# Four closings of a two-layer backbone rebuilt: gate rows from SBUF, units prepared early, token tiles in a pipeline

## The chip, the cores and the metric

The kernel runs on one core of a Trainium2 chip. The metric is the device time of one execution in microseconds (us), the median of several runs; lower is better. Engines are named as in the profile: PE (TensorE), DVE (VectorE), ACT (ScalarE), POOL (GpSimd), SP (SyncE, which issues most DMAs).

## The reference, cut to what matters

Two layers work on 128 context tokens and 256 latent tokens, 384 rows of 2048 values. Context and latent rows have different modulation vectors (group 0 and group 1).

```python
def trunk_layer(x, cvec, ctx_kv, lp):
    mods = jnp.split(silu(cvec) @ lp['w_ada'] + lp['b_ada'], 6, axis=-1)
    sh1, sc1, g1, sh2, sc2, g2 = ...
    h = rms_norm(x, g_pre1) * (1 + sc1) + sh1
    z = h @ w_in                          # 2048 -> 3072
    ...                                   # attention | pooling | convolution, 2048 wide
    mix = concat([attn, pool, conv]) @ w_out
    x = x + g1 * rms_norm(mix, g_post1)   # closing 0 (layer 0), closing 2 (layer 1)
    h = rms_norm(x, g_pre2) * (1 + sc2) + sh2
    f = square(relu(h @ w_mlp1)) @ w_mlp2 # 2048 -> 8192 -> 2048
    x = x + g2 * rms_norm(f, g_post2)     # closing 1 (layer 0), closing 3 (layer 1)
```

## The kernel before, in words

**Matrix products.** Every weight is f32 and is split into a high part `w_hi` (ACT, L558) and a low part `w_lo` (DVE, L840); activations are split in the same way (`h_hi`, `h_lo`). A product is three matmuls (high by high, low by high, high by low). Weights come in units of 512 KB, four units make a quad, and four SBUF slots hold raw, high and low parts. SP loads a unit into `raw` when the low part of the unit four before it is made; ACT may overwrite a slot of `w_hi` when PE has used its unit. So the order of the work is a chain of counting semaphores (`raw_landed`, `hi_ready`, `lo_ready`, `unit_used`) between instruction streams that are written out by hand for each engine.

**Closings.** The second half of the output projection (closings 0 and 2) and the last eighth of the MLP (closings 1 and 3) end in a closing, numbered `r`. It consists of four quads, one for each 512 output columns `n`; PE computes for three token tiles `t` into the banks 4, 5 and 6 of PSUM (`unit_all`, `unit_tok`, L1412). The last quad is done tile by tile, so that tile 0 is ready first. DVE adds the earlier part of the sum (`add_f`, L880), ACT squares it and sums the squares (`square_f`, L587), DVE multiplies by the gate (`gate_f`, L890). The gate is one number for each column, and it is needed along the free dimension: PE makes it in the banks 0 to 3 by eight matmuls for each quad (`gates`, L1433), which broadcast the coefficients of 4 times 128 columns for both groups. Then, for each tile: the root of the mean (`sum_squares_f`, `root_f`), `update_x` (L906, x plus the scaled result, four instructions), the squares of x (`square_x`, L598, four), the root again, and a diagonal matrix with the inverse (`norm_x`, L924). PE turns the tile by multiplying with that diagonal (`turn_x`, L1479, 16 matmuls for each tile in four groups `g`), into the banks 0, 1, 4 and 5 for every tile. ACT (g 0 and 2, L610) and DVE (g 1 and 3, L931) apply scale and shift into `full` (`modulate`), ACT makes `h_hi` (`norm_high`, L617) and DVE `h_lo` (`norm_low`, L939). The next stage's first units wait for the low parts of tile 2 (`h_wait`) and for their own `w_lo`. Closing 3 ends with `update_x` and the output DMAs.

DVE's order in `close_stage` is: everything of tile 0 up to its diagonal, then tile 1, then tile 2 mixed with the modulation of tile 0, then low parts, and behind them the four `w_low` of the next stage's first quad, of which the first stands behind the first low part of tile 2. In `turn_x`, PE runs seven matmuls of 512 columns after tile 0, five after tile 1 and one after tile 2, whose results nobody reads (`keep_warm`, L1467).

**Modulation of layer 1.** While PE runs layer 0's MLP, DVE computes blocks of 512 modulation values of layer 1 with scaled additions (`ada_products`, L1303 and L1305), then a transpose and a sum (L1310, L1314); each of the eight chunks of layer 0's MLP makes three blocks (`WIDE_BLOCKS`). The last of them, block 19 (a part of `sc2`, first used in closing 2), is made beside the last two quads of closing 1.

**Attention.** In each of 24 steps for each layer, `mix` (L1710) multiplies the turned probabilities with the values, for two heads `e` of 64 columns each and for one key block (8 steps) or three (16 steps). The outputs of the two heads lie in different halves of the partitions. The key blocks of head 0 come first, then those of head 1.

## Time and profile before

| | us |
|---|---|
| median of 3 runs (3293.91 to 3299.91) | 3294.25 |
| the profiled execution, its own time | 3297.66 |
| its span, first to last instruction | 3295.9 |
| PE busy | 3207.6 (97%) |
| DVE busy | 2166.7 (66%) |
| ACT busy | 1119.6 (34%) |
| POOL busy | 182.5 (6%) |
| mean DMA rate | 172 GB/s |

All positions below are microseconds from the start of the span. Layer 0's attention ends near 562, closing 0 runs from there to 653, closing 1 from about 1674 to 1761, closing 2 from about 2135 to 2222, and closing 3 from about 3233 to the end. An f32 matmul stands in the trace as two records (two passes), a matmul of split parts as one.

### The profile page before, as it was taken

The page shows a single profiled execution, that of the slowest core. Times are in us where ns is not written, and L with a number is a line of the kernel's source. Part 1 is how long each engine was busy: PE and PEld are TensorE (multiplying, and loading weights), DVE is VectorE, ACT ScalarE, POOL GpSimd, SP SyncE. Part 2 cuts the span into 40 slices and gives each one's busy share as a digit, 9 for nine tenths or more (in the row PEclk, how much of TensorE's full clock was granted, in tenths as well). Part 3 has the DMA queues.
Part 4 walks back from the last instruction along what each step waited for, and adds up shares of the span by engine and source line. Part 5 has one row for each costly group of instructions (what it writes and reads, how often), then busy time and mean ns, then how long its engine had stood idle before and what let it go on. Part 6 is the DMA issues. An engine that isn't in the chain of part 4 may idle for free.

```text
span 3295.9 us, 48061 instructions
## 1 busy us (share of the span) xinstructions
PE 3207.6 (97%) x17289; PEld 2776.6 (84%) x17289; DVE 2166.7 (66%) x3119; ACT 1119.6 (34%) x1567; POOL 182.5 (6%) x211
## 2 busy tenths in 40 slices
PE   7999999999999999999999999999999999999999
PEld 2688656798898998989988986679889899898897
DVE  2366655698988989889895887566546453433335
ACT  2222333532332333323334334353233233332332
POOL 0020132000000000000000303300000000000000
PEclk9999999999999999999999999999999999999999
DMA  9866574277666766766653341225545544344342
GB/s 354 278 199 196 166 237 144 74 232 232 220 223 211 234 212 205 229 223 228 218 173 112 116 129 54 71 63 188 177 128 177 163 142 128 128 127 127 127 128 103
DMA packets 403637, 566.38 MB, mean 172 GB/s; under 512 B 17688, under 2 KB 243600, under 8 KB 403120
## 3 DMA queue, kind: packets, MB, share of 16 engines
q1 hardware_dynamic: 401216, 560.02, 52.2%
q0 software_dynamic: 1344, 4.33, 0.4%
q8 instruction: 75, 1.23, 0.2%
q14 instruction: 58, 0.48, 0.0%
q10 hardware_dynamic: 944, 0.32, 0.0%
HBM read 560.93 MB, written 3.67 MB: 171 GB/s over the span
## 4 chain that ended last, share of the span: by engine, by line
PE 85%; DVE 7%; issue 3%; ACT 3%; DMA 2%; SPq 0%; DVEq 0%; ACTq 0%
PE ps L1404 42%; PE ps L1412 35%; DVE ada_sums L1305 2%; DMA ada_raw<-in_w_ada_dram 1%; PE ps L1501 1%; DVE w_lo L840 1%; PE ps L1524 1%; PE ps L1710 1%; PE ps L1595 1%; PE ps L1684 1%; PE ps L1698 1%; DVE conv L1090 1%; PE ps L1433 1%; ACT facc L598 1%; ACT w_hi L558 1%
## 5 line engine op out<-in xcount | busy, mean ns | idle before, releaser
L840 DVE TENSOR_TENSOR w_lo<-raw,w_hi 128x1024 fp32r<-128x1024 f32 x672 | 826.6, 1234 | 767.8 <-ACT w_hi L558 740.8
L558 ACT ACTIVATE w_hi<-raw 128x1024 fp32r<-128x1024 f32 x672 | 711.7, 1060 | 1472.4 <-PE ps L1412 780.2
L1404 PE MATMUL ps<-h_hi,w_hi 128*128 128x384 f32 x2752 | 929.1, 338 | 7.1 <-DVE w_lo L840 6.2
L1404 PE MATMUL ps<-h_hi,w_lo 128*128 128x384 f32 x2752 | 922.4, 335 | 0.0
L1404 PE MATMUL ps<-h_lo,w_hi 128*128 128x384 f32 x2752 | 922.4, 335 | 0.0
L1412 PE MATMUL ps<-w_hi,hid_hi 128*128 128x512 f32 x1536 | 600.7, 391 | 2.6 <-DVE facc L1325 2.6
L1412 PE MATMUL ps<-w_lo,hid_hi 128*128 128x512 f32 x1536 | 598.1, 389 | 0.0
L1412 PE MATMUL ps<-w_hi,hid_lo 128*128 128x512 f32 x1536 | 598.0, 389 | 0.0
L1305 DVE SCALAR_TENSOR_TENSOR ada_sums<-ada_raw,cond,ada_sums 128x512 f32<-128x512 f32 x840 | 575.9, 749 | 0.0
L1404 PEld LDWEIGHTS ps<-h_hi,w_hi 128*128 128x128 f32 x2752 | 518.5, 188 | 22.9 <-issue 11.5
L1404 PEld LDWEIGHTS ps<-h_lo,w_hi 128*128 128x128 f32 x2752 | 518.6, 188 | 1.1
L1404 PEld LDWEIGHTS ps<-h_hi,w_lo 128*128 128x128 f32 x2752 | 518.6, 188 | 0.0
L1412 PEld LDWEIGHTS ps<-w_hi,hid_hi 128*128 128x128 f32 x1536 | 288.3, 188 | 64.6 <-DVE facc L1325 5.5
L1412 PEld LDWEIGHTS ps<-w_lo,hid_hi 128*128 128x128 f32 x1536 | 288.3, 188 | 60.1
L1412 PEld LDWEIGHTS ps<-w_hi,hid_lo 128*128 128x128 f32 x1536 | 288.4, 188 | 58.8
L1412 PE MATMUL ps<-w_hi,h_hi 128*128 128x512 f32 x384 | 163.0, 424 | 0.0
L1412 PE MATMUL ps<-w_lo,h_hi 128*128 128x512 f32 x384 | 152.0, 396 | 0.0
L1412 PE MATMUL ps<-w_hi,h_lo 128*128 128x512 f32 x384 | 151.9, 396 | 0.0
L1090 DVE SCALAR_TENSOR_TENSOR conv<-glu,pc,conv 128x384 f32<-128x384 f32 x240 | 141.8, 656 | 0.0
L1325 DVE TENSOR_TENSOR facc<-facc,ps 128x512 f32<-128x512 f32 x168 | 115.2, 686 | 31.0 <-PE ps L1412 29.1
L795 ACT ACTIVATE z<-ps 128x768 f32<-128x768 f32 x64 | 52.3, 817 | 202.7 <-PE ps L1404 202.7
L1412 PEld LDWEIGHTS ps<-w_hi,h_hi 128*128 128x128 f32 x384 | 73.4, 191 | 38.0 <-issue 21.5
(201 smaller groups left out, 2094.8 us busy)
## 6 DMA issues: line engine op xcount, KB each, us to landing
raw<-in_w_mlp_dram SPq DMA_DIRECT2D x512, 512.0 KB, 4.0
ada_raw<-in_w_ada_dram SPq DMA_DIRECT2D x360, 512.0 KB, 4.6
raw<-in_w_in_dram SPq DMA_DIRECT2D x96, 512.0 KB, 4.7
raw<-in_w_out_dram SPq DMA_DIRECT2D x64, 512.0 KB, 3.8
ada_aside<-in_w_ada_dram SPq DMA_DIRECT2D x24, 512.0 KB, 10.5
out_dram<-x SPq DMA_DIRECT2D x6, 512.0 KB, 2.7
x<-in_x_sample_dram SPq DMA_DIRECT2D x1, 2048.0 KB, 10.1
pw_w<-in_w_conv_pw_dram POOLq DMA_DIRECT2D x2, 1024.0 KB, 7.8
```

The source lines that it names most:

```text
L558: nc.scalar.activation(w_hi[:, j % 4, :, :], raw[:, j % 4, :, :], ACT.Copy).then_inc(hi_ready, 1)
L598: nc.scalar.activation(facc[:, place(n), t, :], x[:, t, NC * n:NC * n + NC], ACT.Square, accum_out=ss_x[:, t, n:n + 1]).then_inc(x_squared, 1)
L795: nc.scalar.activation(z[:, 16:18, :], ps[:, 2 * pair:2 * pair + 2, 0:TOK], ACT.Relu).then_inc(acc_free, 1)
L840: nc.vector.tensor_tensor(w_lo[:, j % 4, :, :], raw[:, j % 4, :, :], w_hi[:, j % 4, :, :].bitcast(F32), ALU.subtract).then_inc(lo_ready, 1)
L1090: op = nc.vector.scalar_tensor_tensor(out=out, in0=src, scalar=w, in1=out, op0=ALU.mult, op1=ALU.add)
L1305: op = nc.vector.scalar_tensor_tensor(out=out, in0=src, scalar=by, in1=out, op0=ALU.mult, op1=ALU.add)
L1325: nc.vector.tensor_tensor(dst, dst, ps[:, BANK_ACC + t, :], ALU.add).then_inc(acc_added, 1)
L1404: last = nc.tensor.matmul(ps[:, 2 * pair + t, 0:TOK], w[:, j % 4, k, P * t:P * t + P], v[:, kt + k, :], start=begin and k == 0 and i == 0, ...
L1412: last = nc.tensor.matmul(ps[:, BANK_ACC + t, :], v[:, kt + k, tokens(t)], wide(w, j)[:, k, :], start=begin and k == 0 and i == 0, stop=en ...
L1433: last = nc.tensor.matmul(ps[:, 2 * (n % 2) + g, P * i:P * i + P], coef[:, k, 4 * n + i, g:g + 1].to_broadcast([P, P]), ident[:, :], start ...
L1501: last = nc.tensor.matmul(ps[32 * g:32 * g + 32, BANK_ADA, 0:UC], cond[:, 4 * j + g, :], ada_raw[:, j, g, :], start=j == 0, stop=j == 3)
L1524: last = nc.tensor.matmul(ps[32 * g:32 * g + 32, ADA_FIRST[n % 2], :], cond[:, 2 * u + k, :], wide(ada_aside if n >= 2 and u >= 4 else ada ...
```

## The change

- The gate rows are made once per closing. PE transposes the 32 rows of gate coefficients by one matmul (`turn_gates`), DVE copies them to SBUF, ACT's queue stores them in DRAM (16 KB) and loads them back spread over all partitions, 1 MB for each group (`spread_gates`). For closings 0 and 2 they lie in `ada_raw`, for 1 and 3 over `h_hi` and `h_lo`. `gates` with its 64 records for each closing is gone. Because of the place, SP's first modulation load of a layer's MLP waits for the last `gate_f` of the closing ahead of it.
- Three units of the last quad go to spare tiles `e_hi`, `e_lo` (over `h_hi`, `h_lo`), so that the usual slots take the next stage's first three units during the last quad, on ACT and DVE.
- The output banks alternate (4 to 6, 0 to 2), and `turn_x` has banks of its own for each tile; its waits are fewer.
- DVE and ACT take the tiles in a pipeline: the sum of x's squares and the diagonal of tile t come behind the `add_f` and `gate_f` of tile t + 1. `update_x` has three instructions, `square_x` two.
- The low parts of tiles 0 and 1 are made by POOL (`early_lows`), those of tile 2 by DVE.
- `keep_warm` is gone.
- Block 19 moves from closing 1 to the first two pairs of blocks of layer 1's input projection (`late_products`).
- In `mix`, the loop over key blocks is outside and the loop over heads inside.

The diff, cut to its core:

```diff
+F_BANKS = (4, 0, 4, 0)
+TURN_BANKS = ((4, 5, 6, 3), (0, 1, 2, 4), (5, 6, 3, 4))
+TURN_FREED = ((None, None, None, None), (None, None, None, (0, 0)), ((0, 1), (0, 2), (0, 3), (1, 3)))
...
         @block.sync
+                                if first_chunk and halves[k] == 0 and j == 0:
+                                    sp.wait_ge(gate_done, 12 * (2 * layer + 1))
                                 load_ada_wide(layer, lo, i, halves[k], j)
...
         @block.gpsimd
+            def early_lows(p):
+                for t in range(2):
+                    for g in range(4):
+                        kts = slice(4 * g, 4 * g + 4)
+                        pool.wait_ge(gate_done, 12 * p)
+                        pool.wait_ge(norm_hi, 12 * (p - 1) + 4 * t + g + 1)
+                        nc.gpsimd.tensor_tensor(h_lo[:, kts, tokens(t)], full[:, kts, tokens(t)], h_hi[:, kts, tokens(t)].bitcast(F32),
+                                                ALU.subtract).then_inc(early_lo, 1)
...
         @block.scalar
+            def spread_gates(r):
+                act.wait_ge(rows_stored, 16 * (r + 1))
+                for g in range(2):
+                    act.dma_start(gates_by[r % 2][g][:, :], gate_rows[r, g:g + 1, :].to_broadcast([P, D])).then_inc(gates_landed, 16)
+            def last_quads(r, q0):
+                for n in range(3):
+                    for j in range(4):
+                        spare = n == 2 and j < 3
+                        if not spare:
+                            act.wait_ge(unit_used, 4 * (q0 + n) + j + 1)
+                        w_high(j, q0 + n + 1, e_hi if spare else None)
+                    for t in range(TT):
+                        square_f(r, n, t)
...
             def close_stage(r, q, layer, k, shift):
                 p = r + 1
-                for t in range(2):
+                for j in range(3):
+                    act.wait_ge(unit_used, 4 * (q - 1) + j + 1)
+                    w_high(j, q + 1)
+                square_f(r, 3, 0)
+                root_f(r, 0)
+                square_x(r, 0)
+                for t in (1, 2):
                     square_f(r, 3, t)
+                    root_x(p, t - 1)
                     root_f(r, t)
                     square_x(r, t)
-                    root_x(p, t)
...
+                modulate(p, 0, 0, layer, k, shift)
                 root_x(p, 2)
+                modulate(p, 0, 2, layer, k, shift)
+                act.wait_ge(unit_used, 4 * q + 4)
+                w_high(3, q + 1)
                 for g in range(4):
                     norm_high(p, 0, g)
...
         @block.vector
             def close_stage(r, before, layer, k, shift, q):
                 p = r + 1
+                for j in range(3):
+                    w_low(j, q)
+                add_f(r, 3, 0, before)
+                gate_f(r, 3, 0)
+                sum_squares_f(r, 0)
+                update_x(r, 0)
+                for t in (1, 2):
                     add_f(r, 3, t, before)
                     gate_f(r, 3, t)
+                    sum_squares_x(r, t - 1)
                     sum_squares_f(r, t)
+                    norm_x(p, t - 1)
                     update_x(r, t)
                 dve.wait_ge(coefs_ready, 2 * r + 2)
                 modulate(p, 0, 1, layer, k, shift)
+                sum_squares_x(r, 2)
                 modulate(p, 0, 3, layer, k, shift)
                 norm_x(p, 2)
-                for g in range(4):
-                    norm_low(p, 0, g)
                 modulate(p, 1, 1, layer, k, shift)
-                norm_low(p, 1, 0)
                 modulate(p, 1, 3, layer, k, shift)
-                for g in range(1, 4):
-                    norm_low(p, 1, g)
+                w_low(3, q)
                 modulate(p, 2, 1, layer, k, shift)
                 norm_low(p, 2, 0)
-                w_low(0, q)
                 modulate(p, 2, 3, layer, k, shift)
                 for g in range(1, 4):
                     norm_low(p, 2, g)
-                    w_low(g, q)
...
         @block.tensor
-            def gates(r, n, k):
...
+            def turn_gates(r, k, bank, col):
+                pe.wait_ge(coefs_ready, 2 * r + 1)
+                nc.tensor.matmul(ps[0:2 * DT, bank, col:col + P], coef[:, k, :, :].rearrange("p n g -> p (n g)"), ident[:, :],
+                                 start=True, stop=True).then_inc(gates_turned, 1)
...
-            def keep_warm(n, bank):
-                for i in range(n):
-                    nc.tensor.matmul(ps[:, bank, :], ident[:, :], cond[:, :, :].rearrange("p a b -> p (a b)"), start=True, stop=True)
...
             def h_wait(p, j):
-                pe.wait_ge(norm_lo, 12 * (p - 1) + 8 + j + 1)
+                pe.wait_ge(early_lo, 8 * (p - 1) + 4 + j + 1)
+                pe.wait_ge(norm_lo, 4 * (p - 1) + j + 1)
...
                 def mix(s):
-                    for e in range(2):
-                        for i, vb in enumerate(blocks):
+                    for i, vb in enumerate(blocks):
+                        for e in range(2):
                             last = nc.tensor.matmul(ps[64 * e:64 * e + 64, 3, 256:384], vt[:, vb, HD * kv:HD * kv + HD],
                                                     prob_t[:, s % 2, i, P * e:P * e + P], start=i == 0, stop=i == len(blocks) - 1)
```

## Rows read from the trace of the kernel before

**Rows 1.** The profile's page, part 4: the chain that ended last, by engine.

```profile
PE 85%; DVE 7%; issue 3%; ACT 3%; DMA 2%; SPq 0%; DVEq 0%; ACTq 0%
```

**Rows 2.** Windows: us, then busy us (instructions) of PE, PEld, DVE, ACT, POOL, granted clock, DMA share, GB/s.

```profile
450.00:530.00 80.00, 80.00 (x613) 49.73 (x612) 45.32 (x120) 26.58 (x81) 26.44 (x23) 1.00 0.73 236
...
608.00:653.00 45.00, 40.83 (x213) 30.90 (x211) 32.86 (x75) 33.09 (x83) 0.00 (x0) 1.00 0.04 13
```

**Rows 3.** PE's timeline in the tail of closing 0: start, us, line, count.

```profile
608.15 1.95 PE L1433 MATMUL ps<-ident,coef 128*128 128x128 f32 x16
609.85 0.48 PE L1412 MATMUL ps<-w_hi,h_hi 128*128 128x512 f32 x1
...
626.29 3.73 PE L1479 MATMUL ps<-diag,x 128*128 128x128 f32 x32
...
652.97 0.69 PE L1404 MATMUL ps<-h_hi,w_hi 128*128 128x384 f32 x1 [2.51 <-DVE w_lo L840]
```

**Rows 4.** DVE's timeline in closing 0: start, us, line, operation, count, idle before.

```profile
574.30 1.88 DVE L890 TENSOR_TENSOR facc<-facc,ps 128x512 f32<-128x512 f32 x3
...
615.61 0.69 DVE L880 TENSOR_TENSOR facc<-ps,mix_t 128x512 f32<-128x512 f32 x1 [3.15 <-PE ps L1412]
...
625.64 2.08 DVE L906 SCALAR_TENSOR_TENSOR x<-facc,inv_f,x 128x512 f32<-128x512 f32 x3
...
639.28 0.29 DVE L924 TENSOR_SCALAR diag<-ident,inv_x 128x128 f32<-128x128 f32 x1
...
651.09 0.69 DVE L939 TENSOR_TENSOR h_lo<-full,h_hi 128x512 fp32r<-128x512 f32 x1
651.70 1.22 DVE L840 TENSOR_TENSOR w_lo<-raw,w_hi 128x1024 fp32r<-128x1024 f32 x1
```

**Rows 5.** ACT's timeline in closing 0.

```profile
638.95 1.14 ACT L617 ACTIVATE h_hi<-full 128x512 fp32r<-128x512 f32 x2
...
641.98 1.99 ACT L558 ACTIVATE w_hi<-raw 128x1024 fp32r<-128x1024 f32 x2
643.88 1.49 ACT L610 ACTIVATE full<-ps,mods,coef 128x128 f32<-128x128 f32 x4
```

**Rows 6.** Closing 1, timeline: DVE's last modulation products, and PE.

```profile
1722.16 1.22 DVE L1314 TENSOR_REDUCE cond<-flipped 128x32 f32<-128x1024 f32 x1
...
1725.09 0.69 DVE L880 TENSOR_TENSOR facc<-ps,facc 128x512 f32<-128x512 f32 x1
...
1712.86 1.95 PE L1433 MATMUL ps<-ident,coef 128*128 128x128 f32 x16
...
1761.55 0.45 PE L1404 MATMUL ps<-h_hi,w_hi 128*128 128x384 f32 x1 [1.16 <-DVE w_lo L840]
```

**Rows 7.** POOL's groups by form: busy us, mean ns of one.

```profile
L534 POOL TENSOR_TENSOR prob<-prob,small 128x768 f32<-128x768 f32 x32 | 63.2, 1974 | 119.9 <-DVE small L1214 119.9
...
L540 POOL TENSOR_TENSOR h_lo<-o_sb,h_hi 128x128 fp32r<-128x128 f32 x48 | 22.0, 459 | 49.2 <-ACT h_hi L750 48.2
```

**Rows 8.** DMA issues: KB each, median us to landing.

```profile
x<-in_x_sample_dram SPq DMA_DIRECT2D x1, 2048.0 KB, 10.1
```

**Rows 9.** PE's timeline in layer 0's attention: turns (L1698) and mixes (L1710).

```profile
483.08 0.44 PE L1698 MATMUL ps<-ident,prob 128*128 128x128 f32 x2
...
485.95 1.14 PE L1710 MATMUL ps<-prob_t,vt 128*64 128x128 f32 x12
...
490.18 0.87 PE L1698 MATMUL ps<-ident,prob 128*128 128x128 f32 x6
...
493.72 0.44 PE L1710 MATMUL ps<-prob_t,vt 128*64 128x128 f32 x4
```

**Rows 10.** Windows around low stretches of PE's clock, columns as in rows 2.

```profile
649.40:653.00 3.60, 1.09 (x5) 0.26 (x4) 3.60 (x8) 3.57 (x10) 0.00 (x0) 1.00 0.02 5
653.00:656.40 3.40, 3.40 (x11) 3.40 (x12) 3.40 (x7) 1.13 (x2) 0.00 (x0) 0.50 0.59 187
...
2110.50:2120.70 10.20, 7.41 (x24) 5.51 (x23) 4.00 (x8) 1.57 (x3) 3.24 (x3) 0.50 0.30 103
```

More of the change, by code:

```diff
@@ L395, in _ @@
                 else:
-                    with sp.Fori(0, 2) as i:
-                        load_blocks(layer, w_in, quad(layer, Q_IN) + i * 2, CA0 * P + i * 2 * UC, None)
+                    for b in range(2):
+                        for u in range(8):
+                            load_unit(u, quad(layer, Q_IN) + 2 * b, part(w_in, layer, 512 * (u % 4), CA0 * P + 2 * b * UC + UC * (u // 4)))
+                            if u % 2 == 0:
+                                load_ada_late(b, u // 2)
                 for k, tile in enumerate((PU0, K0)):
@@ L1066, in _ @@
                 else:
-                    with dve.Fori(0, 2) as i:
-                        eight_units(quad(layer, Q_IN) + i * 2)
+                    late0 = chain.n
+                    for b in range(2):
+                        eight_units(quad(layer, Q_IN) + 2 * b, None, {2 * j: [lambda b=b, j=j: late_products(b, j, late0)] for j in range(4)})
+                    chain.n = late0 + 24
+                if not first:
+                    block_mods(wide_before(0, 4, 3, 2), 1, 4 * LATE_BLOCK)
                 dve.wait_ge(sig_ready, layer + 1)
@@ L1276, in _ @@
                                 add_f(2 * layer, n, t, first_half)
-                        w_low(j, q + 1)
+                        w_low(j, q + 1, n == 2 and j < 3)
                     for t in range(TT):
@@ L1325, in add_acc, with mlp_quad @@
                     nc.vector.tensor_tensor(dst, dst, ps[:, BANK_ACC + t, :], ALU.add).then_inc(acc_added, 1)
-                def mlp_quad(lo, i, k, mark0, adds=None):
-                    ch, halves, turns = i + lo, half_of_quad(layer, lo), turn_of_quad(layer, lo)
-                    products = k + 1 in halves
-                    late = products and k >= 4
+                def mlp_quad(lo, i, k, mark0, adds=None, blocks=3):
+                    ch, halves, turns = i + lo, half_of_quad(layer, lo, blocks), turn_of_quad(layer, lo, blocks)
+                    with_products = k + 1 in halves
+                    late = with_products and k >= 4
                     for j in range(4):
@@ L1338, in mlp_quad @@
                                 ada_products(lo, i, halves[k + 1], 2, mark0)
-                        w_low(j, ch * Q_CHUNK + quad(layer, Q_MLP + k + 1))
+                        w_low(j, ch * Q_CHUNK + quad(layer, Q_MLP + k + 1), blocks < 3 and k == 6 and j < 3)
                         if k < 3 and j == 3:
                             hidden_low(2 * k, ch * 4 + (k + 32 * layer))
-                        if products and not (late and j == 2):
+                        if with_products and not (late and j == 2):
                             ada_products(lo, i, halves[k + 1], j, mark0)
@@ L1406, in unit, with unit_tok, unit_all @@
                 last.then_inc(unit_used, 1)
-            def unit_tok(j, q, kt, hi, lo, t, begin, end):
+            def unit_tok(j, q, kt, hi, lo, t, begin, end, bank=BANK_ACC, spare=False):
+                high, low = (e_hi, e_lo) if spare else (w_hi, w_lo)
                 for k in range(2):
-                    for i, (v, w) in enumerate(((hi, w_hi), (lo, w_hi), (hi, w_lo))):
-                        last = nc.tensor.matmul(ps[:, BANK_ACC + t, :], v[:, kt + k, tokens(t)], wide(w, j)[:, k, :],
+                    for i, (v, w) in enumerate(((hi, high), (lo, high), (hi, low))):
+                        last = nc.tensor.matmul(ps[:, bank + t, :], v[:, kt + k, tokens(t)], wide(w, j)[:, k, :],
                                                 start=begin and k == 0 and i == 0, stop=end and k == 1 and i == 2)
                 return last
-            def unit_all(j, q, kt, hi, lo, free, done):
+            def unit_all(j, q, kt, hi, lo, free, done, bank=BANK_ACC):
                 pe.wait_ge(lo_ready, 4 * q + (j + 1))
```

338 lines of the change are left out of this document (169 added, 169 removed).

## The prediction

> **What bounds the kernel now.** I read the chain that ended last first: PE has 85% of it, DVE 7%, ACT 3% [rows 1]. So the kernel is bound by matmuls nearly everywhere, and a change pays in two ways: by matmuls that go, and by stretches in which the chain leaves PE. Then the windows by stage. In the tail of closing 0 PE is busy 40.8 of 45.0 us, but most of that are turns and products that nobody reads, while DVE and ACT are busy 33 us each [rows 2]: a chain of both bounds it. In the attention, PE is busy 80 of 80 us between 450 and 530 [rows 2]. Last, the timelines of the three tails on each engine, to see what PE's next stage waits for: in closing 0 the first unit's `w_lo` [rows 3, 4], in closing 1 the same after an earlier backlog on DVE [rows 6].
>
> I count each tail from the end of the third quad. In closing 0 that is 608.15, and the next stage begins at 652.97: 44.8 us [rows 3]. Closing 2 has the same steps and takes as long. In closing 1 it is 1712.86 to 1761.55, 48.7 us [rows 6].
>
> **Gate groups: 22.1 us gained.** Four closings of four quads have 16 gate groups, of 16 records each [rows 3]. One holds PE from 608.15 to 609.85, 1.70 us [rows 3], and nothing runs beside it on PE. Three groups lie inside the tails and are counted there. The other 13 are on the path: 13 x 1.70 = 22.1. What they could have hidden, the low part of unit 3, has three units of lead.
>
> **The tail of closings 0 and 2: 5.8 us each.** Steps from 0 = end of the third quad, durations from closing 0 [rows 4, 5].
> - PE does tile 0 of the last quad without a gate group in front, ready at 5.7. DVE first ends the third quad (one addition, `w_low` of unit 3, three gates: to 4.2), and now has three `w_low` of the next stage before tile 0. Each holds it for 1.13 (1.22 less an overlap of 0.1 [rows 4]): 4.2 + 3.4 = 7.6. Before, tile 0 began at 615.61, that is 7.5. Nothing is gained here, DVE is late instead of PE.
> - Before, the three tiles took from 615.61 to the third diagonal at 639.28, 23.7 us [rows 4], because DVE waited for ACT's squares and roots twice for each tile. Now the addition and gate of the next tile (1.3) lie over the squares of x. What is left for a tile: 1.3, two pairs of small sums with ACT's roots 1.3, reciprocals and diagonal 0.3, and the update, one instruction of 1024 at 1.2 and two of 512 at 0.67 (2.08 for three [rows 4]), 2.5: 5.4 in all. The first tile takes 5.7, as ACT loads its table for the root there. Tile 2's update ends at 7.6 + 5.7 + 5.4 + 5.4 = 24.1. Two modulations of 1.3, the sum of squares and the diagonal bring 27.2.
> - From there ACT is the chain: a modulation 1.4, `w_high` 1.0, four high parts 2.1, two modulations 2.8, four high parts 2.1, a modulation 1.5, a high part 0.6 [rows 5], begun at 26.8: 38.2. DVE's low part adds 0.7, and `w_lo` is no longer behind it (it was, from 651.70 [rows 4]). PE starts at 39.0. Before, 13.7 us lay between the third diagonal and the start; now 11.8.
>
> 44.8 - 39.0 = 5.8, twice: 11.6.
>
> **The tail of closing 1: 10.6 us.** DVE still worked on block 19 until about 1723.3, 10.5 us after the third quad [rows 6], so tile 0's addition came at 1725.09, 12.2 instead of 7.5. With the block gone, the steps are those above, less 0.9 for a table that is loaded only after the attention's exponentials: 38.1. 48.7 - 38.1 = 10.6. The moved work is 32 products of 0.69 and 2.5 us of transpose and sum, 25 us on DVE beside 16 units of the input projection. A quad's matmuls take 16.4 (609.85 to the first turn at 626.29 [rows 3]), a unit 4.1; the projection's units have as many columns to stream, and DVE has only 1.13 of its own in each. Its eight loads stand in SP's queue between weight loads that are three units ahead. I cost it at nothing; without that cover PE would wait the difference.
>
> **Attention: 7.0 us.** A mix of one key block is four records and takes 0.44, just what two turn records take in sequence (0.44) [rows 9]: the two heads run side by side. A mix of three blocks takes 1.14, where six records in sequence take 0.87 [rows 9]: head 1 joins late. With the heads alternating I expect 0.87, 0.27 less. That holds for 32 steps at most (8.6) and for none if DVE's steps bound it. I take 26 steps, as PE has no idle time in the middle of the attention [rows 2] but has some at either end: 7.0.
>
> **What is added: 2.0 us.** Four transposes on PE, 0.37 each by the turns above, 1.5, and DVE's copy of a gate block ahead of the attention, at most 0.3 twice. ACT's twelve DMA issues have no row; ACT waits for PE or DVE where they stand, and I take nothing, at most 1 us each for the four stores. The spread rows are 2 MB; the nearest load, 2048 KB, took 10.1 [rows 8]. Issued at the attention's end near 562 they land near 574, when DVE wants the first of them (574.30 [rows 4]). DVE has `w_low` queued behind that wait, with three units, 12 us, of lead for PE. In closings 1 and 3 they are asked for earlier still against the first gate. SP's wait for the last gate blocks weight units that are needed 30 us later. Nothing for both.
>
> **POOL's low parts.** POOL's instruction of 128x512 has no row. By width from the one of 768 (1.97) it is 1.3, by four times the one of 128 (0.459) it is 1.8 [rows 7]; I take 1.5. The first starts at 29.8; the fifth, for which PE waits, ends at 37.3, before 39.0. The Trainium skill, page "GPSIMD Engine Reference", section "8. Key points", says that GpSimd shares its SBUF interfaces with VectorE and contends with instructions of two SBUF inputs. That speaks against this part; it is weighed among the rivals.
>
> **PE's clock: 4.1 us lost.** After a stretch of 3.6 us with PE busy for 1.09, the granted clock was 0.50 for 3.4 us [rows 10], 1.2 GHz instead of 2.4, and the first 3.4 us of the MLP cost 1.7 too much. So `keep_warm` did not prevent it. Without them PE is idle for some 7 us before the start. The longest low stretch here is 10.2 us with PE busy for 7.4 [rows 10]. I take 5 us at the low level after each of the three tails, 2.5 lost: 0.8 more than before in closings 0 and 2, and 2.5 in closing 1, whose next stage began at full clock (0.45 for its first matmul [rows 6] against 0.69 [rows 3]). Ends: nothing, and 5.1 a tail, 12 more in all. The turns at the low level take some 7 instead of 3.7 us (626.29 [rows 3]), which ACT's queue hides.
>
> The Trainium skill, page "TensorE: Matmul & The Clock Gate", section "Why this matters for your kernels", says to leave no long idle gap between matmuls, as the clock falls back to half. By that rule alone `keep_warm` is worth what it costs; by the rows it costs nothing but time in which PE waits, and it had not held the clock.
>
> **Sum.** 22.1 + 11.6 + 10.6 + 7.0 + 0.1 (closing 3's shorter last update) - 2.0 - 4.1 = 45.3. The profiled execution took 3297.66 (span 3295.9), so a like execution would take 3252.4. It lies 3.4 above the median of the runs, 3294.25, from which I take the forecast: 3249.
>
> **Rivals.**
> - *As forecast*, own range 3244 to 3255: 0.63.
> - *The mix gains nothing*, because DVE's softmax steps end last. For: PE waited for DVE at both ends. Against: 80 of 80 us. 3256; 0.13.
> - *POOL becomes the bound.* From 1.9 us an instruction PE waits for its fifth; contention with DVE could do it. At 2.6 us the fifth ends at 42.8, 3.8 late, three times: 3260. Against: POOL's rows were taken beside a working DVE. 0.07.
> - *The gate rows arrive late*, beyond the 12 us of lead, in closings 0 and 2. Ten us beyond it twice: 3269. Against: rows 8, and a DMA share of 0.04 in the tail [rows 2]. 0.05.
> - *Slower: the clock stays low.* Without the extra products PE has turns of 3.7 us between idle stretches, then a next stage at 1.2 GHz. It turns the sign if each of three starts loses 16.5 us, 33 us at the low level; at 40 us each 3304. Against: the longest stretch is 10.2 us, and steady matmuls followed by full clock each time [rows 10]. 0.04.
> - *More is gained:* clock as before, all 32 mixes, 3243; 0.08.
>
> The range 3240 to 3264 leaves out the late rows, the clock and the worst of POOL. About 0.2% (6.6 us) is what a measurement of this kernel tells from no change. Faster 0.95, same 0.01, slower 0.04.
>
> **What would show it.** No L1433 groups in any closing; third quad's end to the next stage's first matmul 39 us (38 in closing 1); three diagonals 5.4 apart; mixes of 0.87; POOL's low parts of 1.3 to 1.9 us; clock 0.50 for some 5 us at the three starts. I am wrong if PE waits for `h_lo` of POOL, if DVE idles for a DMA before its first gate, or if the attention keeps its length.

## The result

The changed kernel takes **3253.86 us** (median of 4 runs, 3252.09 to 3258.6), the one before 3294.08 (4 runs, 3293.77 to 3299.91). The ratio is 0.9876, with a 95% interval from 0.9859 to 0.9893. The forecast was 3249, and 3253.86 lies in its range. The two profiled executions differ by more than the medians: 3297.66 and 3253.25 us, 44.4 less (forecast 45.3), where the medians differ by 40.2: the profiled execution of before lay 3.6 us above the median of its runs, that of after 0.6 below.

The chain that ended last, by engine, answers to [rows 1]; PE has one point more.

```profile
PE 86%; DVE 6%; issue 3%; ACT 2%; DMA 2%; DVEq 0%; SPq 0%; ACTq 0%
```

To see where the 44 us came from, I cut both traces at the same events: the first matmul of a closing's first quad, of its last quad, and of the next stage. The gate group of the last quad lies in the second row, ahead of the tail. Stage lengths in us:

| stage | before | after | difference |
|---|---|---|---|
| to the first quad of closing 0 | 547.73 | 544.22 | -3.5 |
| quads 1 to 3 of the four closings | 237.95 | 208.95 | -29.0 |
| tails of closings 0, 1, 2 (last quad to next stage) | 43.12, 46.99, 43.12 | 39.00, 38.08, 38.99 | -17.2 |
| MLP of layer 0, layer 1 | 1005.05, 993.13 | 1006.82, 993.46 | +2.1 |
| layer 1: next stage to first scores | 229.02 | 236.51 | **+7.5** |
| layer 1: first scores to closing 2 | 125.01 | 120.97 | -4.0 |
| last quad of closing 3 | 16.22 | 16.09 | -0.1 |

Two rows are longer with the change: the input stage of layer 1 by 7.5 us, and the two MLPs by 2.1, of which 1.1 is low clock at their starts (below).

**The tail of closing 0.** PE's timeline, to be read beside [rows 3]: the last quad follows the third at once, the turns come in three batches, and PE then stands for 5.93 us until DVE's low part.

```profile
599.43 0.39 PE L1490 MATMUL ps<-e_hi,h_hi 128*128 128x512 f32 x1
...
615.76 3.73 PE L1540 MATMUL ps<-diag,x 128*128 128x128 f32 x32
620.79 2.94 PE L1540 MATMUL ps<-diag,x 128*128 128x128 f32 x24 [1.30 <-DVE diag L1020]
626.17 6.33 PE L1540 MATMUL ps<-diag,x 128*128 128x128 f32 x40 [2.43 <-ACT full L676]
638.43 0.68 PE L1481 MATMUL ps<-h_hi,w_hi 128*128 128x384 f32 x1 [5.93 <-DVE h_lo L1035]
```

DVE's timeline there, beside [rows 4]: the three early `w_low` first, then tile 0; the table load shows as 1.17 us of waiting for ACT; the diagonals are 5.3 and 5.9 us apart.

```profile
603.68 3.48 DVE L901 TENSOR_TENSOR w_lo<-raw,w_hi 128x1024 fp32r<-128x1024 f32 x3
607.08 0.68 DVE L976 TENSOR_TENSOR facc<-ps,mix_t 128x512 f32<-128x512 f32 x1
...
610.07 0.16 DVE L997 RECIPROCAL inv_f<-std_f 128x1 f32<-128x1 f32 x1 [1.17 <-ACT std_f L657]
...
615.16 0.29 DVE L1020 TENSOR_SCALAR diag<-ident,inv_x 128x128 f32<-128x128 f32 x1
...
620.45 0.29 DVE L1020 TENSOR_SCALAR diag<-ident,inv_x 128x128 f32<-128x128 f32 x1
...
626.38 0.29 DVE L1020 TENSOR_SCALAR diag<-ident,inv_x 128x128 f32<-128x128 f32 x1
...
637.47 0.69 DVE L1035 TENSOR_TENSOR h_lo<-full,h_hi 128x512 fp32r<-128x512 f32 x1 [5.65 <-ACT h_hi L683]
```

The last row also shows who ends the tail: DVE had nothing to do for 5.65 us and waited for ACT (the engine named in the brackets), which after the third diagonal still had a `w_high`, three groups of modulations and nine high parts to do.

**The input stage of layer 1.** DVE's timeline, then PE's, at the end of block 19.

```profile
1799.54 2.73 DVE L932 SCALAR_TENSOR_TENSOR ada_sums<-ada_raw,cond,ada_sums 128x512 f32<-128x512 f32 x4
1802.31 1.25 DVE L937 STREAM_TRANSPOSE flipped_in<-ada_sums 128x1024 f32<-128x1024 f32 x1
1803.59 1.22 DVE L941 TENSOR_REDUCE cond<-flipped_in 128x32 f32<-128x1024 f32 x1
```

```profile
1801.09 0.34 PE L1481 MATMUL ps<-h_hi,w_lo 128*128 128x384 f32 x1
1804.86 0.25 PE L1606 MATMUL ps<-cond,fold 128*32 128x8 f32 x8 [3.44 <-DVE cond L941]
1805.18 0.68 PE L1481 MATMUL ps<-h_hi,w_hi 128*128 128x384 f32 x1
```

PE's stream has the block's small product right behind the sixteenth unit, and DVE has its sum 5.3 us after it began the last four products. So PE stands for 3.44 us, and after that a full matmul of 384 columns takes 0.68 us where it took 0.34.

**The clock.** Windows (columns as in [rows 2]) at the starts after closings 0, 1 and 2, and before and after the wait for block 19. All low windows are at 0.50 of the clock, 1.2 GHz.

```profile
637.70:644.50 6.80, 6.07 (x19) 6.08 (x20) 4.59 (x8) 2.69 (x7) 4.93 (x3) 0.50 0.00 0
1730.00:1736.80 6.80, 4.06 (x13) 4.07 (x14) 4.82 (x8) 4.68 (x12) 4.86 (x4) 0.50 0.01 2
1798.00:1805.00 7.00, 3.56 (x28) 3.25 (x26) 6.54 (x8) 3.76 (x5) 0.00 (x0) 1.00 0.32 96
1805.00:1808.50 3.50, 3.43 (x18) 3.35 (x14) 3.22 (x6) 1.12 (x1) 1.57 (x3) 0.51 0.35 109
2184.00:2187.40 3.40, 2.85 (x9) 2.86 (x10) 3.40 (x7) 2.51 (x6) 2.66 (x2) 0.50 0.00 0
```

Of the three starts 6.1, 4.1 and 2.8 us lie at the low level, which costs half of it, 6.5 us. Before, 3.4 us lay there after closings 0 and 2 each and nothing after closing 1, which cost 3.4 us. So the clock takes 3.1 us more at the starts, and 1.7 in the input stage: 3.44 + 1.7 there, and 2.05 at its start, are 7.2 of the 7.5 us. Five more executions with the same wait (e2 to e6) have 3.4 us of low clock too, beginning within 1.3 us of the wait's end.

**POOL and the mix.** Two groups of the page.

```profile
L509 POOL TENSOR_TENSOR h_lo<-full,h_hi 128x512 fp32r<-128x512 f32 x24 | 34.3, 1461 | 1214.5 <-ACT h_hi L683 1214.5
```

```profile
L1766 PE MATMUL ps<-prob_t,vt 128*64 128x128 f32 x448 | 36.9, 294 | 11.2 <-DVE prob_t L1324 8.0 <-DVE prob_t L1326 3.3
```

POOL's low part takes 1.46 us on the average. The mix has the same 448 records of the same length, but busy time in which two overlap counts once, and that fell from 45.1 to 36.9 us. One mix of three blocks, to be read beside [rows 9], where it took 1.14:

```profile
483.82 0.88 PE L1766 MATMUL ps<-prob_t,vt 128*64 128x128 f32 x12
```

### The profile page after: what moved, and what is told of

Read it like the earlier page. It is cut to its first block, busy times and chain, and to the rows that moved or that the text cites. A ratio compares the mean times of both kernels' runs of the same rounds, so it can differ in the third digit from the quotient of the medians.

```text
span 3251.5 us, 46826 instructions
## 1 busy us (share of the span) xinstructions
PE 3144.4 (97%) x16963; PEld 2730.0 (84%) x16963; DVE 2151.5 (66%) x3087; ACT 1110.8 (34%) x1531; POOL 216.1 (7%) x235
## 4 chain that ended last, share of the span: by engine, by line
PE 86%; DVE 6%; issue 3%; ACT 2%; DMA 2%; DVEq 0%; SPq 0%; ACTq 0%
PE ps L1481 42%; PE ps L1490 35%; PE ps L1555 1%; PE ps L1578 1%; DVE w_lo L901 1%; DVE ada_sums L932 1%; DMA ada_raw<-in_w_ada_dram 1%; PE ps L1649 1%; DVE conv L1190 1%; PE ps L1740 1%; PE ps L1754 1%; PE ps L1766 1%; PE ps L1727 1%; ACT full L676 1%; DVE x L1002 1%
## 5 line engine op out<-in xcount | busy, mean ns | idle before, releaser
L901 DVE TENSOR_TENSOR w_lo<-raw,w_hi 128x1024 fp32r<-128x1024 f32 x660 | 810.3, 1232 | 739.7 <-ACT w_hi L601 718.3
L601 ACT ACTIVATE w_hi<-raw 128x1024 fp32r<-128x1024 f32 x660 | 697.8, 1059 | 1459.0 <-PE ps L1490 757.9
L1490 PE MATMUL ps<-w_hi,hid_hi 128*128 128x512 f32 x1500 | 586.0, 391 | 2.6 <-DVE facc L1403 2.6
L1490 PE MATMUL ps<-w_hi,hid_lo 128*128 128x512 f32 x1500 | 584.0, 389 | 0.0
L1490 PE MATMUL ps<-w_lo,hid_hi 128*128 128x512 f32 x1500 | 584.0, 389 | 0.0
L1490 PEld LDWEIGHTS ps<-w_hi,hid_hi 128*128 128x128 f32 x1500 | 281.5, 188 | 63.4 <-DVE facc L1403 5.5
L1490 PE MATMUL ps<-w_hi,h_hi 128*128 128x512 f32 x348 | 148.4, 426 | 0.0
L1490 PE MATMUL ps<-w_lo,h_hi 128*128 128x512 f32 x348 | 138.5, 398 | 0.0
L1490 PE MATMUL ps<-w_hi,h_lo 128*128 128x512 f32 x348 | 138.3, 397 | 0.0
L1403 DVE TENSOR_TENSOR facc<-facc,ps 128x512 f32<-128x512 f32 x168 | 115.0, 685 | 30.4 <-PE ps L1490 28.5
L509 POOL TENSOR_TENSOR h_lo<-full,h_hi 128x512 fp32r<-128x512 f32 x24 | 34.3, 1461 | 1214.5 <-ACT h_hi L683 1214.5
## 6 DMA issues: line engine op xcount, KB each, us to landing
x<-in_x_sample_dram SPq DMA_DIRECT2D x1, 2048.0 KB, 10.1
```

What stands on the lines that cost most here:

```text
L509: nc.gpsimd.tensor_tensor(h_lo[:, kts, tokens(t)], full[:, kts, tokens(t)], h_hi[:, kts, tokens(t)].bitcast(F32), ALU.subtract).then_inc(e ...
L601: nc.scalar.activation(dst[:, j % 4, :, :], raw[:, j % 4, :, :], ACT.Copy).then_inc(hi_ready, 1)
L901: nc.vector.tensor_tensor(low[:, j % 4, :, :], raw[:, j % 4, :, :], high[:, j % 4, :, :].bitcast(F32), ALU.subtract).then_inc(lo_ready, 1)
L1403: nc.vector.tensor_tensor(dst, dst, ps[:, BANK_ACC + t, :], ALU.add).then_inc(acc_added, 1)
L1490: last = nc.tensor.matmul(ps[:, bank + t, :], v[:, kt + k, tokens(t)], wide(w, j)[:, k, :], start=begin and k == 0 and i == 0, stop=end an ...
```

## The experiments

Besides its time each gave a trace. Where no interval is given, the time is that of a single execution. The start of closing 0 varies by up to 5.3 us between executions of kernels that are the same up to there, so small edits behind it are compared by one length: from closing 0's first quad to the last product, 2739.6 us before and 2698.9 after. "Tails" are those of closings 0, 1 and 2.

### e1: block 19's small product later

PE's small product goes two units further on, DVE's addition behind it (in place of both right behind the sixteenth unit).

```diff
-                    turn_sums(wide_before(0, 4, 3, 2))
...
+                    two_blocks(quad(layer, Q_IN + 4), blk(layer, B_IN + 4), None, after={1: lambda: turn_sums(wide_before(0, 4, 3, 2))})
```

> Layer 1's input stage, from its first matmul to the first score, took 229.0 us before and 236.5 with the change. PE now waits 3.44 us for the fold of block 19 right after the first two pairs of blocks, and the clock is low for 3.4 us after it. Here that small product on PE stands two units later and DVE takes the sum in another unit later; nothing else differs. Theory (the moved block costs by where PE turns it): no wait of PE at L1606, no low clock there, the stage 3.4 + 1.7 = 5.1 us shorter, 231.4; the whole 3248. Rival (DVE's added products or their eight loads slow the stage): the wait moves to w_lo or to a raw load and the stage stays within 1 us of 236.5.

3250.01 us (before, on the same chip: 3293.51). No wait is left at the small product, the input stage is 232.8 us instead of 236.5, tails 39.0, 38.1, 39.0, the length 2695.6, 3.3 less. That is 3.7 less in the stage where I had expected 5.1: the low stretch behind the wait is gone, but one of 3.4 us lies at 1947, near the stage's end, where the changed kernel has none. In e8 and e11, with the same edit, the stage takes 231.1 and 230.9 us. So the wait was the moved block's, and it does not come back behind. This is the term that I had at nothing.

### e2: TensorE busy ahead of the start

```diff
+                pe.wait_ge(mods_ready, (ADA_BLOCKS, ADA_BLOCKS + ADA_WIDE - 1, ADA_BLOCKS + ADA_WIDE)[p - 1])
+                for i in range(6):
+                    nc.tensor.matmul(ps[:, BANK_ADA, :], ident[:, :], x[:, 2, 0:NC], start=True, stop=True)
```

behind the turn of tile 2; nobody reads the results.

> Six products of 512 columns that nobody reads are put behind tile 2's turn in each of three closings, into PE's idle 6 to 8 us before the next stage. With the change the next stages began at half clock and lost 6.1, 4.1 and 2.8 us of low clock, some 6.5 us in all against full clock. Theory (PE's idleness before the start costs that): the clock is at full level at the three starts, 5 to 6.5 us gained, with the tails as long as before (39.0, 38.1, 39.0). Rival (as in the kernel before, such products do not hold the clock, or delay the start because they run at half clock themselves): gain under 2 us, or tails 1 to 4 us longer.

3251.74 us; the length is 2696.1, 2.8 less, of which I had expected more. The low clock at the starts was 3.4 us in closing 0, 3.4 in closing 1 and none in closing 2. The products help, but where the low stretches fall still differs between closings. The tails are 40.1, 38.1 and 39.0; the 1.1 too much in closing 0 comes back under e6.

### e8, and e11 with more runs: e1 and e2 together

> The late turn of block 19 and the six products before each next stage together. If both act and do not meet, 5 + 5 us less than the changed kernel: profiled 3242 to 3245. Rival: the products before the start bring nothing, 3248.

3248.17 us, where I had expected 3242 to 3245: by the time alone the rival (3248) would hold. But closing 0 began 3.5 us later than in the changed kernel's profile, in code that is the same, and behind it the length is 2690.3, 8.5 less. There was no low clock at the starts after closings 0 and 1 and 3.4 us of it around the one after closing 2; tails as in the changed kernel. The two parts together give more than their single sums, 3.3 and 2.8. Because one execution can lie well, it was timed again:

> The kernel of e8 a second time, now timed against the kernel before: block 19's small product and its addition later, and six unread products after the third tile's turn. From its one profile (8.5 us less than the changed kernel between the first quad of closing 0 and the last product): 0.9850 of the time before, some 3245 us where the changed kernel has 3253.9. If the 8.5 us are only where that one execution happened to lie with its stretches at the lower clock, its time is that of the changed kernel within 2 us (0.9876).

3247.52 us (3245.01 to 3248.49) against 3295.28, ratio 0.9852, from 0.9837 to 0.9867; the length of its profile is 2690.9, again 8 less. I had expected 0.9850. The interval overlaps that of the changed kernel (0.9859 to 0.9893) by a little; the two profiles agree on the gain in length.

### e7: the kernel before without its unread products

`keep_warm` and the two waits ahead of it are taken out of the kernel before; nothing else.

> The kernel before without keep_warm alone: 13 products of 512 columns less in each of three closings. Theory (they cost nothing, since DVE and ACT bound the tails, and hold nothing): tails of 44.8, 48.7, 44.8 within 0.5 us; low clock of 3.4 to 7 us at each next start, so 0 to 5 us slower in all. Rival (they delayed the turns and so the tail): tails over 1 us shorter. Rival (they held the clock): over 8 us slower.

3290.32 us (before: 3296.82). Tails 43.05, 46.93, 43.05 (before 43.12, 46.99, 43.12), the length 2737.6, 2.0 less. So the thirteen products cost nothing and held nothing: PE ran them while it waited. With them two of the three starts had low clock, without them only the one after closing 1. I had expected 0 to 5 us more; of the 6.5 us less in the time, 5.3 lie ahead of closing 0, where the code is the same. In closing 0 the low stretches lie in the tail, and the clock is full at the start (two windows, columns as in [rows 2]):

```profile
639.20:646.00 6.80, 5.10 (x24) 5.13 (x25) 4.91 (x13) 6.74 (x18) 0.00 (x0) 0.50 0.00 0
648.30:651.70 3.40, 3.36 (x19) 3.36 (x20) 3.40 (x7) 1.19 (x3) 0.00 (x0) 1.00 0.62 178
```

### e3: the gate groups' load put back

Sixteen times 16 records into a bank that nobody reads, at the place where `gates` stood.

```diff
+                for g in range(2):
+                    for i in range(4):
+                        nc.tensor.matmul(ps[:, 3, P * i:P * i + P], coef[:, k, 4 * n + i, g:g + 1].to_broadcast([P, P]), ident[:, :],
+                                         start=True, stop=True)
```

> The changed kernel with 16 groups of eight broadcast products put back where the gate groups stood; they write bank 3 and nobody reads them, the gates still come from SBUF. Theory (the groups were pure time of PE): each quad's length grows by 1.70 to 1.78 us, 27 to 28.5 in all, of which the one inside each tail comes back only in part, as DVE and not PE begins tile 0 at 7.6: tails 0 to 0.5 longer counted from the third quad's end. Whole 3275 to 3282. Rival (the gain came from other things, such as the alternating banks, and PE's groups were hidden): under 10 us.

3277.66 us; the length is 2722.1, 23.2 more. From a closing's first quad to its last it takes 7.0 to 7.2 us more for four groups, 1.75 to 1.80 each and 28.5 in all. From the third quad's end the tails are 39.0, 38.5 and 39.0, that is, the group inside a tail costs nothing, or 0.4 in closing 1, because DVE is late there anyway.

### e4: the old order of the mix

```diff
-                    for i, vb in enumerate(blocks):
-                        for e in range(2):
+                    for e in range(2):
+                        for i, vb in enumerate(blocks):
```

> Only the order of the two loops in mix is put back: all key blocks of head 0, then those of head 1. Theory (the heads run side by side only when they alternate): a mix of three blocks takes 1.14 us instead of 0.87, and as PE is bound in the attention most of it comes back: the two attention stages 6 to 8 us longer together, the whole 3260. Rival (DVE's softmax steps bound the attention): mixes of 1.14 but the stages within 2 us of the changed kernel's.

3260.74 us (before: 3293.51). From the first to the last scores layer 0 takes 158.3 us instead of 155.4 and layer 1 115.5 instead of 112.1, 6.3 in all. The tail of closing 0 is 40.1 (see below, "POOL and DVE hold each other off"). The mix of three blocks, in e4:

```profile
483.32 1.14 PE L1766 MATMUL ps<-prob_t,vt 128*64 128x128 f32 x12
```

The 6.3 us hold for this pair of traces. The other kernels differ in the attention by this order alone, so their traces serve as repeats. From first to last scores, with the part at the low clock in brackets:

| | layer 0 | layer 1 |
|---|---|---|
| old order: before, e4, e7 | 158.3 (3.4), 158.3 (3.4), 156.9 (0) | 115.9 (2.8), 115.5 (2.2), 114.5 (0) |
| new order: the changed kernel | 155.4 (3.4) | 112.1 (0) |
| new order: the ten other experiments | 156.9 to 157.4 (6.8 to 8.3) | 112.0 to 112.1 (0) |

With half of each low part taken off, the old order has 156.6 to 156.9 and 114.4 to 114.5, the new one 153.1 to 153.7 and 112.0 to 112.1: the alternation is worth about 3.3 us in layer 0 and 2.4 in layer 1, 5.7 together. In layer 0 most of it was lost again to the clock in ten of eleven executions, and the changed kernel's profile happened to be the eleventh. Whether the new order itself brings the longer low part is not shown.

### e5: the early low parts back on VectorE

`early_lows` is gone; DVE makes the eight low parts of tiles 0 and 1 between its modulations.

> The low parts of tiles 0 and 1 go back from POOL to DVE, in the order of the kernel before; the rest is the changed kernel. POOL's instruction took 1.46 us, DVE's takes 0.69 (0.6 apart). Theory (DVE and ACT together bound the tail, so eight instructions less on DVE pay in part): by the steps of the prediction the modulation of tile 2 on DVE comes later and the next stage starts 2.5 us later: tails of 41.5, 40.6, 41.5 instead of 39.0, 38.1, 39.0. Rival (ACT alone bounds the tail): tails unchanged within 0.3 us.

3264.9 us; tails 41.5, 40.6, 41.5, the length 2706.8, 7.95 more. The step sums of the prediction hold to a tenth.

### e6: the tiles one after the other

`close_stage` of DVE and ACT without the pipeline over tiles; all else as changed.

```diff
-                for t in (1, 2):
-                    add_f(r, 3, t, before)
-                    gate_f(r, 3, t)
-                    sum_squares_x(r, t - 1)
-                    sum_squares_f(r, t)
-                    norm_x(p, t - 1)
-                    update_x(r, t)
+                for t in range(3):
+                    add_f(r, 3, t, before)
+                    gate_f(r, 3, t)
+                    sum_squares_f(r, t)
+                    update_x(r, t)
+                    if t < 2:
+                        sum_squares_x(r, t)
+                        norm_x(p, t)
```

> The changed kernel with the tiles one after the other on DVE and ACT again: each tile's diagonal before the next tile's addition. (PE also waits for tile 2's addition before it turns tile 1, because of a shared bank.) Theory by the steps of the prediction: third diagonal 3.6 us later (30.8 instead of 27.2 after the third quad), tails of 42.6, 41.7, 42.6: three times 3.6, 11 us in all, 3264. Rival (ACT's modulations bound the tail whatever comes before): tails within 1 us.

3267.96 us (before: 3296.82); the length is 2710.6, 11.7 more. The tails are 43.8, 41.8 and 43.8: closing 1 as expected, the other two 1.2 more. The timeline around the last step of closing 0 shows why:

```profile
642.23 2.48 POOL L509 TENSOR_TENSOR h_lo<-full,h_hi 128x512 fp32r<-128x512 f32 x2
...
643.45 1.81 DVE L1033 TENSOR_TENSOR h_lo<-full,h_hi 128x512 fp32r<-128x512 f32 x1 [4.72 <-ACT h_hi L683]
```

DVE's low part, 0.68 us in other places, begins at the same time as POOL's next one and takes 1.81; PE waits for it. In closing 1 it begins 0.09 us ahead of POOL's and takes 0.69. The difference, 1.1, is what the tails had too much. The tail of 40.1 us in e2 has the same row:

```profile
637.97 1.81 DVE L1035 TENSOR_TENSOR h_lo<-full,h_hi 128x512 fp32r<-128x512 f32 x1 [4.73 <-ACT h_hi L683]
```

### POOL and DVE hold each other off

That calls for the same rows of the others. Each gives the shortest, the median and the longest (ns) of one engine's low parts; DVE's are those of closing 0. First the changed kernel.

```profile
L509 POOL TENSOR_TENSOR h_lo<-full,h_hi x24: 1253/1264/2377, 629.1 to 2185.4; 128x512 fp32r<-128x512 f32 x24
...
L1035 DVE TENSOR_TENSOR h_lo<-full,h_hi x4: 677/685/1703, 637.5 to 641.6; 128x512 fp32r<-128x512 f32 x4
```

Then e5, where DVE makes all twelve and POOL none.

```profile
L1033 DVE TENSOR_TENSOR h_lo<-full,h_hi x12: 681/684/692, 632.0 to 646.0; 128x512 fp32r<-128x512 f32 x12
```

Alone, POOL takes 1.26 us and DVE 0.68. When both want a subtraction of two SBUF tiles, one waits until the other's instruction ends: POOL's longest, 2.37 at 629.11, is 1.26 plus the 1.21 of the `w_low` that DVE began at 629.14, less 0.1; DVE's longest, at 639.38, is 0.68 plus the 1.16 that were left of POOL's, less the same 0.1. The modulations, from PSUM, are not held up: four take 1.36 us at 638.08, beside POOL, and 1.36 at 1717.69, where POOL is idle. The Trainium skill, page "SBUF — State Buffer", section "Who interferes with whom", has this as an exclusive lock that the first to issue keeps for the whole instruction; the trace agrees, but the recorded starts do not always tell who was first (POOL's 629.11 is 0.03 ahead of DVE's 629.14, and POOL was the one held up). In the changed kernel the lock costs nothing, since DVE's first low part of tile 2 began at 637.47, just ahead of a POOL instruction, and POOL had time to spare. A tenth of a microsecond decides that: e8 and e11 are the same code, and closing 2's tail is 39.0 in the one (DVE first) and 40.2 in the other (POOL first, DVE's low part 1.81). It was decided 8 us earlier. In e11 POOL's first low part took 1.27 us, DVE's `w_low`, begun 0.08 behind it, waited for it (2.27), and POOL's second part took 2.25. In e8, as in the changed kernel, `w_low` took 1.21 and POOL's first part 2.37. So POOL was 0.1 us further on in e11, and its seventh part began 0.02 ahead of DVE's low part instead of 0.09 behind it. The rows of e11:

```profile
2168.03 2.27 DVE L901 TENSOR_TENSOR w_lo<-raw,w_hi 128x1024 fp32r<-128x1024 f32 x1
...
2176.32 1.81 DVE L1035 TENSOR_TENSOR h_lo<-full,h_hi 128x512 fp32r<-128x512 f32 x1 [4.74 <-ACT h_hi L683]
```

The longer tails of closing 0 in e2 and e4, and of closings 0 and 2 in e6, have the same two rows.

### e9 and e10: all of tile 1's modulation on VectorE

The room that DVE has before its first low part of tile 2 is used: it takes the groups 0 and 2 of tile 1 from ACT, and does one modulation of tile 2 ahead of `w_low` of unit 3 instead of behind it. e9 is this with e1 and four unread products (e8 has six), e10 the same without unread products.

```diff
+BY_ACT = ((0, 0), (0, 2), (2, 0), (2, 2))
+BY_DVE = ((0, 1), (0, 3), (1, 0), (1, 1), (1, 2), (1, 3), (2, 1), (2, 3))
...
-                modulate(p, 1, 0, layer, k, shift)
-                modulate(p, 1, 2, layer, k, shift)
...
```

> e8 with four unread products in the place of six, and with the two groups of tile 1's modulation that ScalarE had given to VectorE. Theory: between the third diagonal and the next stage ScalarE is the longer of the two (VectorE stands for some 5.8 us ahead of its first low part of tile 2), so work that moves to VectorE shortens each tail by 2.7 us: 36.3, 35.4 and 36.3 us, 8 us in all, and 0.9825 of the time before. Rival: VectorE has no such room because its eight more small operations put off its work on tile 2, or GpSimd's low parts of tile 1 end last: tails of 38 to 40 us, and no gain over e8.

> As e9 without the unread products: e1 with all of tile 1's modulation on VectorE. If the balance of the two engines is worth 2.7 us in each tail, the tails are 36.3, 35.4 and 36.3 us here too, and from the first quad of closing 0 to the last product 2687.5 us (e1: 2695.6). What e9 gains over that, some 4 to 5 us if e8 tells it right, is then the unread products' alone; if the shorter tails leave TensorE less idle, so that the stretch at the lower clock at the next stage's start goes by itself, e9 and this one are within 2 us.

e9: 3240.67 us (3237.02 to 3242.63) against 3295.28, ratio 0.9832, from 0.9819 to 0.9846. Its length is 2682.1, 8.2 less than e8's. The tails are 37.8, 36.9 and 37.8 in e9 and e10, 1.2 less and not 2.7. What ends them is now POOL, in e9:

```profile
628.57 12.52 POOL L511 TENSOR_TENSOR h_lo<-full,h_hi 128x512 fp32r<-128x512 f32 x8 [69.34 <-ACT h_hi L686]
```

```profile
632.35 3.60 PE L1547 MATMUL ps<-x,ident 128*128 128x512 f32 x8
636.68 0.44 PE L1482 MATMUL ps<-h_hi,w_hi 128*128 128x384 f32 x1 [0.73 <-POOL h_lo L511]
```

Eight low parts take 12.52 us where eight at 1.26 would take 10.1. This is the rival "POOL becomes the bound" of the prediction, in a faster tail: DVE's `w_low` and low parts now fall beside POOL's. e10 took 3244.2 us, its length is 2691.0. The 8.9 us between them are not the 4 to 5 that I expected of the unread products. In e10, 3.4 us at the start after closing 0 and some 4 us at each of the other two were at the low level; in e9 none at any of the three. That is 5.9 us. e10 also had low stretches of 3.4 us in the input stage and 3.4 us more around the end of layer 1's attention, which e9 had not, 3.4 us lost. So what the unread products save depends on where the later low stretches fall as well, and e10 is one execution.

### e12: POOL's low parts in the order of their use

```diff
-                for t in range(2):
-                    for g in range(4):
+                for t, g in ((0, 0), (0, 1), (1, 0), (0, 2), (1, 1), (0, 3), (1, 2), (1, 3)):
...
-                pe.wait_ge(early_lo, 8 * (p - 1) + 4 + j + 1)
+                pe.wait_ge(early_lo, 8 * (p - 1) + (3, 5, 7, 8)[j])
```

> e9 with GpSimd's eight low parts in the order in which TensorE wants them (the first group of tile 1 third and no longer fifth) and three unread products in the place of four. Theory: in e9 the next stage began when GpSimd's fifth low part came, a step of 1.56 us each, and VectorE's first low part of tile 2 was there 1.1 us sooner; so now VectorE's sets the start, the tails are 36.7, 35.8 and 36.7 us (e9: 37.8, 36.9, 37.8), and from the first quad of closing 0 to the last product 2679 us (e9: 2682.1), 0.9822 of the time before. Rival: GpSimd's later groups are late instead (its eighth low part at the same time as in e9, with TensorE a unit ahead), and TensorE waits inside the next stage's first units for what it won: shorter tails, but nothing from the first quad to the last product.

**3237.95 us** (3235.49 to 3240.29) against 3297.9, ratio 0.9822, from 0.9808 to 0.9836: the fastest kernel of the study, and 0.0054 below the changed one, whose interval it does not touch. Against e9 the intervals overlap. The tails are 36.7, 36.4 and 36.7; PE waits for DVE again:

```profile
637.13 0.44 PE L1481 MATMUL ps<-h_hi,w_hi 128*128 128x384 f32 x1 [0.50 <-DVE h_lo L1035]
```

In closing 1 the low part was there at 1727.1, but three unread products at the low clock held PE until 1727.97. The length is 2681.1, only 1.0 less than e9's, though the tails give 2.6. I had expected 36.7, 35.8 and 36.7, and 2679. The rival does not hold: after closings 0 and 2 the first 192 matmuls take 33.4 us in both kernels. 1.0 us of what is missing lies within the first 120 us of layer 0's MLP, the rest in parts of 0.2 to 0.3; the cause stays open.

## Why the prediction was right, and where it was not

- **Gate groups, 22.1.** Right. The quads with the sixteen groups are 29.0 us shorter in the traces, and 28.5 come back with the groups (e3), 1.75 to 1.80 each against 1.70. The length grows by 23.2 only, as what lies within the tails hides, which is why the prediction counted 13.
- **Tails, 11.6 and 10.6.** Right to a tenth: from the third quad's end 39.0, 38.1 and 39.0, as forecast. Diagonals came 5.3 and 5.9 apart where I had 5.4; the second distance is longer by the modulation of tile 0 between them. e5 and e6 confirm two steps by taking them back. The units prepared early and the banks of its own for each tile were not taken back by themselves; for them only the sum of the steps speaks.
- **Block 19, at nothing.** This step failed. "Without that cover PE would wait the difference" was right as a sentence, but I compared DVE's load with PE's over the whole stretch and did not look at the end, where PE's small product stands right behind the last unit and DVE's last products, transpose and sum take 5.3 us more. It cost 3.4 us of waiting and 1.7 of clock, 5.1; e1 takes the wait away by moving the product by two units, and got 3.7 of it back in its one trace.
- **PE's clock, 4.1.** 3.1 at the three starts (6.1, 4.1 and 2.8 us low; I had 5, 5, 5), and the 1.7 above. That the unread products had not held the clock is shown by e7. The Trainium skill advises against long idle gaps between matmuls (page "TensorE: Matmul & The Clock Gate", section "Why this matters for your kernels"). These runs agree for products laid right ahead of the start: without them all three starts had low clock (the changed kernel, e1, e3 to e6, e10), with them two in e2 and e11, one in e8 and none in e9 and e12. Those of `keep_warm`, which PE had done 2.5 us before the start [rows 3], bought nothing: two starts with them, one without (e7).
- **Attention, 7.0.** The mechanism was right: a mix of three blocks takes 0.88 instead of 1.14, and 1.14 again in e4. The size agrees in this pair of traces, 2.9 and 3.8 us less from first to last scores, 6.7, but partly by luck: all traces together give 5.7 at full clock, which is 22 mixes at 0.26 and not 26 at 0.27, and most other executions keep less of it in layer 0 (table under e4).
- **POOL, 1.5 us.** Right as an average (1.46), but for another reason: 1.26 alone, near the 1.3 by width, and more when DVE holds it off. The contention that the prediction quotes from the Trainium skill (page "GPSIMD Engine Reference", section "8. Key points") is there in the trace; it did not decide here, and it did in e6 and e9.
- **The gate rows**, at nothing: right. They land in 4.8 and 7.1 us, within the lead. ACT's DMA rows of the change:

```profile
gates_out_ctx<-gate_rows ACTq DMA_DIRECT2D x2, 1024.0 KB, 4.8
gates_out_lat<-gate_rows ACTq DMA_DIRECT2D x2, 1024.0 KB, 7.1
```

The forecast of the pair, 45.3, came within 0.9 of 44.4 partly by luck, because the 5.1 that I missed were mostly made up: the quads gave 23.9 outside the tails and not 22.1, the clock at the starts took 1.0 less, and the added work, for which I had 2.0, shows no length of its own in the table (the 0.37 for a transpose stands in none of the rows; its records take 0.27 to 0.30 each). The median is 4.9 above the forecast: 0.9 of that is the gain, and 4.0 come from the 3.4 us that I took off for an execution of before above its median, while that of after lay 0.6 below its own. Between medians the change gives 40.2 us; how much of the missing 4 us is the attention's clock and how much is scatter, four runs do not tell.

## What to carry to other kernels

When work moves beside a busy engine, check the last instruction of the moved chain against the place where its reader stands, and not only the two loads; here a reader two units later had no wait. When a tail is shortened, look which engine is idle before its last step, move work there, and then look at the order in which the others deliver. The subtractions on POOL and DVE, which both read two SBUF tiles, did not run side by side here, so count such pairs as one queue. And when a gain is read from one pair of traces, look how the same stage did in every other trace that has the same code.

## What the hardware showed that I had not expected

- DVE and POOL take turns by whole instructions: 0.68 becomes 1.70 to 1.81 us, and 1.26 becomes up to 2.4 in the changed kernel and 2.5 in e9. Whether that lengthens a tail by 1.1 us depends on which of the two is first, and it differs between executions of the same code.
- A wait of 3.44 us in the middle of full work was followed by 3.4 us at half the clock, in all six executions that have it. Where such a stretch falls relative to a start moved the length by up to 9 us between kernels that differ by four unread products in each tail (e9, e10).
